# Hybrid attention block on one core: the near-distance bias moves from TensorE to VectorE's copy, and the inverse root to the split of y

## What is computed

```python
def block(args):
    i, qb = args
    dist = _block_dist(i, s)
    bias = rel_bias[_t5_bucket(jnp.maximum(dist, 0))]
    bias = jnp.moveaxis(bias, -1, 0).astype(jnp.float32)
    logits = jnp.einsum('bhqcd,bhkcd->bchqk', qb, k).astype(jnp.float32) * scale + bias
    logits = jnp.where(dist >= 0, logits, NEG)
    p = jax.nn.softmax(logits, axis=-1)
    a = p[:, 0] - lam * p[:, 1]
    return jnp.einsum('bhqk,bhkd->bhqd', a, v32)
...
o_a = _rmsnorm(o_a, diff_head_norm[l]) * (1.0 - lam_init)
...
y = y * jax.nn.silu(gate)
```

## Time and profile before

| | |
|---|---|
| median of 3 runs | 2624.19 us (2621.52 to 2629.36) |
| profiled execution | 2637.26 us, span of its instructions 2635.5 us |
| granted clock of PE, mean | 0.977 |
| PE, PEld busy | 2381.7 us (90%), 1629.8 us (62%) |
| DVE, ACT, POOL busy | 1725.6 us (65%), 1606.3 us (61%), 1335.5 us (51%) |
| diff stages (PE's scores of the kind diff) | 461 to 605, 985 to 1148, 1525 to 1680, 2065 to 2235 us |

### The profile page before, as it was taken

The page is one execution under the profiler, slowest core; times in us unless marked ns, Lnnn a source line. Parts: engine busy times, 40 slices in busy tenths (PEclk is TensorE's granted clock), DMA queues, the critical chain, the costliest instruction groups (busy, mean ns, idle before and its releaser), DMA issues. The chain is left out here.

```text
span 2635.5 us, 72425 instructions
## 1 busy us (share of the span) xinstructions
PE 2381.7 (90%) x27166; PEld 1629.8 (62%) x27166; DVE 1725.6 (65%) x4545; ACT 1606.3 (61%) x4373; POOL 1335.5 (51%) x2128
## 2 busy tenths in 40 slices
PE   5699999999999999979989999799899996799998
PEld 4576666666766666658666665586666654544443
DVE  7646689886556898866559988665588896311121
ACT  5456888566577886656678866566788665311221
POOL 6435555666575566666665666656756455100000
PEclk9799999999999999989999999899999998899999
DMA  6369998745699888356998983558998833764341
GB/s 195 95 119 154 158 160 151 143 87 104 136 181 169 156 143 163 69 107 135 172 171 155 142 167 74 93 123 164 178 158 145 154 69 57 192 167 104 89 112 48
DMA packets 987800, 353.05 MB, mean 134 GB/s; under 512 B 833956, under 2 KB 972204, under 8 KB 987436
## 3 DMA queue, kind: packets, MB, share of 16 engines
q1 hardware_dynamic: 980856, 330.58, 65.4%
q0 software_dynamic: 6592, 17.83, 2.5%
HBM read 72.38 MB, written 35.23 MB: 41 GB/s over the span
## 5 line engine op out<-in xcount | busy, mean ns | idle before, releaser
L1588 POOL TENSOR_TENSOR rows<-rows 128x512 f16<-128x512 f32 (+3 forms) x864 | 861.0, 1011 | 681.1 <-ACT rows L1514 674.9
L1345 PE MATMUL job<-wt,big 128*128 128x128 f16 x10752 | 682.8, 220 | 2.8 <-DVE planes L1603 1.9
L1345 PE MATMUL job<-big,wt 128*128 128x512 f16 x2688 | 665.8, 381 | 10.5 <-PEq L768 5.1
L1345 PEld LDWEIGHTS job<-wt,big 128*128 128x128 f16 x10752 | 628.9, 98 | 46.1 <-DVE planes L1603 3.0
L1514 ACT CAST rows<-rows 128x512 f16<-128x512 f32 (+3 forms) x864 | 458.2, 544 | 242.2 <-DMA rows<-rows 192.8
L1411 PE MATMUL mixed<-values,rows 128*128 128x64 f16 (+1 forms) x8544 | 428.9, 201 | 103.1 <-DMA rows<-rows 79.7
L1411 PEld LDWEIGHTS mixed<-values,rows 128*128 128x128 f16 x8544 | 378.0, 99 | 224.9 <-DMA rows<-rows 118.5
L1535 ACT ACTIVATE rows<-rows,neg_max 128x512 f32<-128x512 f32 (+3 forms) x704 | 445.6, 635 | 109.1 <-DVE neg_max L1649 108.9
L1393 PE MATMUL scores<-stack 128*128 128x512 f16 (+3 forms) x1600 | 435.2, 351 | 42.0 <-DVE rows L1641 31.9
L1641 DVE TENSOR_SCALAR_CACHE_REDUCE rows<-scores 128x512 f32<-128x512 f32 (+3 forms) x704 | 398.6, 590 | 89.4 <-POOL rows L1588 66.5
L1345 PEld LDWEIGHTS job<-big,wt 128*128 128x128 f16 x2688 | 246.6, 98 | 255.6 <-issue 13.5
(11 more groups left out here) (157 smaller groups left out, 2784.0 us busy)
## 6 DMA issues: line engine op xcount, KB each, us to landing
stack<-planes SPq DMA_DIRECT2D x160, 192.0 KB
ws<-w_in SPq DMA_DIRECT2D x56, 512.0 KB, 4.8
y_halves<-y_out_halves SPq DMA_DIRECT2D x64, 256.0 KB, 2.7
rows<-rows SPq DMA_TRANSPOSE x864, 3.3
rows<-x SPq DMA_DIRECT2D x16, 512.0 KB, 5.8
temps<-w_out POOLq DMA_DIRECT2D x64, 128.0 KB, 3.4
out_weight_halves<-temps POOLq DMA_DIRECT2D x64, 128.0 KB, 3.7
big<-out_weight_halves SPq DMA_DIRECT2D x16, 512.0 KB, 10.6
```

Of the source, the lines that this page charges most:

```text
L1345: last = nc.tensor.matmul(dst, lhs, rhs, start=(k0 == 0 and q == 0), stop=(k1 == KT and q == len(pairs) - 1))
L1588: nc.gpsimd.tensor_tensor(halves_of(tau, 1, w), scored(plan.chunk_at(g, m, k0), 0, w), halves_of(tau, 0, w), ALU.subtract).then_inc(low_po ...
```

## The change

The bias is added by DVE: a chunk is copied in up to two pieces, the far one by `tensor_scalar` as before and the near one by `tensor_tensor_reduce`, which adds the fp32 bias from `near_f` and takes the maximum. The three bias matmuls per near chunk, the buffer `near` and `split_near` go. `take` goes: `square` and `post` read the accumulator itself, and the next step's `mix` waits for `post`, as after the other kinds. `post` no longer multiplies by the root; `y_hi` and `y_low` do it as their scale, where the constant 0.5/64 was. The root, its variance, its sum of squares and its first guess get two places each, so `variance` and `inverse_root` wait for steps two back. Three one-element `scalar_tensor_tensor` of DVE (one in `combine`, two in `variance`) become `tensor_scalar`. The planner's numbers are all set anew (of `RANK` only PE's are shown).

```diff
--- before.py
+++ after.py
...
-    "pe": {"mix": 4.37083, "score": 4.93189, "gate": 5.45902, "project": 6.22450},
...
+    "pe": {"mix": 3.42686, "score": 5.99980, "gate": 6.18532, "project": 7.37012},
...
-                need = [("turn", tau)] + ([self.taken_by(g - 1)] if g and at == 0 else [])
+                need = [("turn", tau)] + ([("post", g - 1)] if g and at == 0 else [])
...
         def y_scale(g):
+            if KINDS[g] == "diff":
+                return root[:, DIFF_STEP[g] % 2:DIFF_STEP[g] % 2 + 1]
...
-                            sp.wait_ge(near_step, 5 * lane)
+                            sp.wait_ge(s_free, soft_count(plan.last_chunk[args[0] - len(KIND_ORDER)]))
...
-                        if kind == "diff" and i == 0:
-                            pe.wait_ge(near_step, 5 * (UNIT[t].lane + 1))
...
-                    if kind == "diff":
-                        first = max(c, (i - 1) * P)
-                        if first < c + w:
-                            at, width = first - c, c + w - first
-                            off = first - (i - 1) * P
-                            for a in range(3):
-                                parts.append((at, width, ident_b[:, :], near[:, a, off:off + width]))
...
-                        if KINDS[g - 1] == "diff":
-                            pe.wait_ge(o_copied, DIFF_STEP[g - 1] + 1)
-                        else:
-                            pe.wait_ge(posted, g)
+                        pe.wait_ge(posted, g)
...
-                    if op == "take":
-                        act.wait_ge(pv_done, mixed(g))
-                        if DIFF_STEP[g]:
-                            act.wait_ge(posted, g if KINDS[g - 1] == "diff" else LAST_DIFF[g] + 1)
-                        nc.scalar.copy(o_copy[:, :], o_bank[:, 0:P]).then_inc(o_copied, 1)
                     if op == "y_hi":
                         act.wait_ge(posted, g + 1)
+                        if KINDS[g] == "diff":
+                            act.wait_ge(root_step, (DIFF_STEP[g] + 1) * ROOT)
...
-                        act.wait_ge(o_copied, DIFF_STEP[g] + 1)
-                        nc.scalar.activation(junk[:, :], o_copy[:, :], ACT.Square, accum_out=sc[:, 6:7]) \
+                        d = DIFF_STEP[g]
+                        act.wait_ge(pv_done, mixed(g))
+                        if d >= 2:
+                            act.wait_ge(var_ready, (d - 1) * VAR)
+                        nc.scalar.activation(junk[:, :], o_bank[:, 0:P], ACT.Square, scale=P ** -0.5,
+                                             accum_out=sc[:, 10 + d % 2:11 + d % 2]) \
                             .then_inc(squared, 1)
...
-                    v, y, a, b = sc[:, 2:3], root[:, 0:1], root[:, 1:2], root[:, 2:3]
+                    v, y, a, b = sc[:, 8 + d % 2:9 + d % 2], root[:, d % 2:d % 2 + 1], root[:, 2:3], root[:, 3:4]
                     pool.wait_ge(var_ready, (d + 1) * VAR)
+                    if d >= 2:
+                        y_split(pool, DIFF_ROWS[d - 2])
...
+                def copies(g, c, w):
+
+                    first = (plan.steps[g][1] - 1) * P if KINDS[g] == "diff" else c + w
+                    cut = min(max(first - c, 0), w)
+                    return [(a, b) for a, b in ((0, cut), (cut, w)) if b > a], cut
+
                 def soft_chunk(g, n, m, c, w):
                     r = (2 * g + m) % ROWS
+                    t, i = plan.steps[g]
+                    at = sum(len(copies(g, c0, w0)[0]) for _, r0, c0, w0 in plan.chunks[g] if r0 == m and c0 < c)
                     dve.wait_ge(s_full, n + 1)
                     row_free(dve, n)
-                    nc.vector.tensor_scalar(scored(n, 0, w), s_bank[n % S_BANKS][:, 0:w], 1.0,
-                                            -3.0e38, ALU.mult, ALU.max,
-                                            accum_out=mx[:, r, c // BANK:c // BANK + 1]).then_inc(s_free, 1)
+                    cuts, cut = copies(g, c, w)
+                    if i == 0 and KINDS[g] == "diff":
+                        dve.wait_ge(near_landed, 16 * (UNIT[t].lane + 1))
+                    for q, (a, b) in enumerate(cuts):
+                        peak = mx[:, r, at + q:at + q + 1]
+                        if a < cut:
+                            last = nc.vector.tensor_scalar(scored(n, a, b), s_bank[n % S_BANKS][:, a:b], 1.0,
+                                                           -3.0e38, ALU.mult, ALU.max, accum_out=peak)
+                        else:
+                            off = c + a - (i - 1) * P
+                            last = nc.vector.tensor_tensor_reduce(scored(n, a, b), s_bank[n % S_BANKS][:, a:b],
+                                                                  near_f[:, ::-1][:, off:off + b - a], 1.0, -3.0e38,
+                                                                  ALU.add, ALU.max, peak)
+                    last.then_inc(s_free, 1)
...
-                        nc.vector.scalar_tensor_tensor(sc[:, 1:2], sc[:, 0:1], neg_lam[:, 0:1], z0, op0=ALU.mult,
-                                                       op1=ALU.mult).then_inc(coef_step, 1)
+                        nc.vector.tensor_scalar(sc[:, 1:2], sc[:, 0:1], neg_lam[:, 0:1], z0, ALU.mult, ALU.mult) \
+                            .then_inc(coef_step, 1)
...
-                    z0, v = z_sum[:, col(g, 0)], sc[:, 2:3]
-                    nc.vector.scalar_tensor_tensor(sc[:, 7:8], z0, EPS, z0, op0=ALU.mult, op1=ALU.mult) \
-                        .then_inc(var_ready, 1)
+                    d = DIFF_STEP[g]
+                    var = d * VAR
+                    z0, v, floor = z_sum[:, col(g, 0)], sc[:, 8 + d % 2:9 + d % 2], sc[:, 7:8]
+                    seed = root_i[:, d % 2:d % 2 + 1]
+                    if d >= 2:
+                        dve.wait_ge(root_step, (d - 1) * ROOT)
+                    nc.vector.tensor_scalar(floor, z0, z0, EPS, ALU.mult, ALU.mult).then_inc(var_ready, 1)
...
-                    nc.vector.scalar_tensor_tensor(v, sc[:, 6:7], 1.0 / P, sc[:, 7:8], op0=ALU.mult,
-                                                   op1=ALU.add).then_inc(var_ready, 1)
-
+                    dve.wait_ge(squared, d + 1)
+                    nc.vector.tensor_scalar(v, sc[:, 10 + d % 2:11 + d % 2], floor, None, ALU.add).then_inc(var_ready, 1)
...
-                    if kind == "diff":
-                        dve.wait_ge(o_copied, DIFF_STEP[g] + 1)
-                        dve.wait_ge(root_step, (DIFF_STEP[g] + 1) * ROOT)
-                        nc.vector.scalar_tensor_tensor(y, o_copy[:, :], root[:, 0:1], gate, op0=ALU.mult, op1=ALU.mult) \
-                            .then_inc(posted, 1)
-                        return
                     dve.wait_ge(pv_done, mixed(g))
-                    if kind == "stick":
-                        nc.vector.scalar_tensor_tensor(y, o_bank[:, 0:P], 0.5 / W_SCALE, gate, op0=ALU.mult,
-                                                       op1=ALU.mult).then_inc(posted, 1)
+                    if kind in ("stick", "diff"):
+                        if kind == "diff":
+                            dve.wait_ge(squared, DIFF_STEP[g] + 1)
+                        nc.vector.scalar_tensor_tensor(y, o_bank[:, 0:P], 0.5 / W_SCALE if kind == "stick" else 1.0, gate,
+                                                       op0=ALU.mult, op1=ALU.mult).then_inc(posted, 1)
...
-                def split_near(t):
-                    at = 5 * UNIT[t].lane
-                    dve.wait_ge(near_landed, 16 * (UNIT[t].lane + 1))
-                    if UNIT[t].lane:
-                        dve.wait_ge(s_full, plan.last_chunk[t - len(KIND_ORDER)])
-                    for a in range(3):
-                        nc.vector.tensor_copy(near[:, a, :], near_f[:, ::-1]).then_inc(near_step, 1)
-                        if a < 2:
-                            dve.wait_ge(near_step, at + 2 * a + 1)
-                            nc.vector.tensor_tensor(near_f[:, :], near_f[:, :], near[:, a, ::-1], ALU.subtract) \
-                                .then_inc(near_step, 1)
-                            dve.wait_ge(near_step, at + 2 * a + 2)
```

More of the change, by code:

```diff
@@ L58 @@
 RANK = {
[L59 to L70 removed]
+    "pe": {"mix": 3.42686, "score": 5.99980, "gate": 6.18532, "project": 7.37012},
+    "act": {"beta": -1.02044, "convert": 0.09860, "square": 1.56409, "y_hi": 1.90013, "stick": 4.11322,
+            "job": 4.42739, "hi": 4.85840, "exp": 6.05197},
+    "dve": {"lo_dve": 1.52081, "weigh": 1.69925, "ylo": 1.93750, "combine": 2.12124, "low": 2.34038,
+            "post": 3.72902, "scan": 4.02979, "norm": 6.33521, "widen": 6.61046, "copy": 7.20142},
+    "pool": {"lo": 0.09877, "wo": 2.26711, "ylo_pool": 2.95644, "root": 4.79189},
+    "sp": {"stacks": -0.49115, "store": 1.06927, "pairs": 1.90869, "sums": 2.46883, "turn": 2.93844,
+            "strip": 7.81310, "near_in": 13.10196},
+}
+AHEAD = {"mem": 1.00000, "stick": 0.75620, "diff": 0.14564, "forget": 0.68448}
+SLACK, LATE = 17.35582, 11.80560
 MARGIN = {
```

(20 more changed lines are left out.)

68 lines of the change are left out of this document (24 added, 44 removed).

## The result

The changed kernel took **2602.45 us** (median of 4 runs, 2597.89 to 2605.17) beside 2626.77 (2621.52 to 2629.36) of the kernel before on the same chip: ratio 0.9908, 95% interval 0.9885 to 0.9931. That is 24 us less; the forecast was 47 us less.

The account below looks back on a forecast made before the run. PE, busy 90% of the span, was taken as the bound. From the 2624.19 us median, -40.4 (bias matmuls) - 13 (VectorE's relief) + 6 (moved waits) = -47.4 gave 2577 us; range 2550 to 2612.

Parts of the forecast that it names:

- second case: Rival, 0.20: VectorE gives nothing back, as small tensor_scalars still wait for POOL or add-and-reduce is dear; 2590, up to 2610.
- The bias matmuls at 40.4 us: Diff stages on PE: removing 456 bias matmuls, 95,232 columns at 0.424 ns, saves 40.4 us; ends 20 and 66.2.
- No change: Rival, 0.06: the chain score, copy, exp, combine, transpose, mix sets each diff step, so freed time is waiting; about 2622.
- VectorE's relief at 13 us: Diff stages: 58 us less work on DVE shortens PE's 38.7 us of waits for copies by a third, 13 us.
- (b): DVE's chunk copies: chunks straddling the near tiles' border are cut in two, 88 more instructions, costing 8 us in all.
- (c): DVE's 152 near pieces: add-and-reduce taken to cost no more than the plain copy; other end 30 us.
- (d): DVE's three one-element operations per diff step, as tensor_scalar at 0.154 us: 79.4 us become 29.6, 49.8 us less.
- (e): DVE's y product, reading PSUM and no longer the root: 34.2 us become 18.0 at 0.281 us each, 16.2 us less.
- The waits that move: First mix matmul after a diff step now waits for square and product, not ACT's copy: adds 6 us; ends 0 and 32.
- The replanned order: Job parts newly placed around PE's 7.98 us bubble before the mem stage: taken as 0, with 15 us either way.
- Slower: Rival, 0.07: the next mix waits for the product queued behind exp and copy, 1.8 us later; 2629; decides from 0.83 us a step.
- The signs named in advance: PE busy some 40 us lower, DVE 58; variance operations 150 to 160 ns; PE's product wait under 10 us, copy waits about 26.

Follow-up runs that it names:

- run 1: Kernel before without its 456 bias matmuls, nothing else touched, so the near-distance bias is left out: 2611.75 us, ratio 0.9938.
- run 12: Kernel before with bias added by VectorE, small sums as tensor_scalar, root at y's split, take removed, 63 operations moved in the old order: 2822.74 us, 1.0743.
- run 3: Kernel before with only the three one-element operations per diff step turned into tensor_scalar: 2614.64 us, ratio 0.9941.
- run 5: Kernel before, in its old order, with bias added by VectorE and the three small sums as tensor_scalar, nothing else: 2591.95 us, ratio 0.9851.
- run 2: Kernel before, in its old order, with only the bias part changed (VectorE adds the bias as it copies, two bias buffers): 2609.36 us, ratio 0.9930.
- version 9: Kernel before with bias added by VectorE, small sums as tensor_scalar and root at y's split; take kept, old order: 2588.92 us, ratio 0.9843.

## Why the prediction was wrong

The sign, the range (2550 to 2612) and the band of the second case (2590 to 2610) held the time. That case held it by luck: of its mechanism, small sums that still wait for POOL or a dear add-and-reduce, nothing came. The forecast was 25 us too low; it promised 47 us and the change gave 24, and two terms carry that.

- **The bias matmuls at 40.4 us: the first step that failed.** As time they gave 16 us alone (run 1), below even the lower end of 20. As work the figure was high too: PE's busy time fell by 31.4 us in run 1 and by 26 to 40 in the other profiles without these matmuls, run 12 apart. Busy time of PE was read as path because PE was at 91%; as far as the waits show, in the diff stages the chain score, copy, exp, combine, mix sets the pace for part of the time: PE's waits for copies rose by 14 us (58.4 to 72.1). That was the rival given 0.06 ("No change"), half true.
- **VectorE's relief at 13 us** was about right: the small sums alone gave 15 (run 3), and 21 on top of the bias part (run 5 against run 2). Bias and relief together gave 39 to 41 (runs 5, 9), where the two terms said 53.4, so 12 to 14 us are missing, and they are the bias matmuls'. The reason given, that the stalls stand right ahead of copies, held: in run 3 PE's waits for copies fell by 15 us. The 38.7 us of such waits were counted to 2240 us in the last stage; to 2235, where the stage ends, they are 31.7, which changes nothing here.
- **(b) and (c)**: right. 418 and 285 ns are the copy's line, and run 2 equals run 1. **(d)**: the 154 ns was too low for sums that read a pointer (203, 214, 273 ns: 44 us, not 29.6), but the rival behind it didn't come. None of them was held up in 64 executions each (at most 274 ns, at L1674), though 44 (L1698), 44 (L1701) and 31 (L1674) of them began while a POOL operation ran; the old L1688 took up to 1153. The Trainium skill (VectorE: DVE Perf Modes, Mode 2×_2P; SBUF — State Buffer, Who interferes with whom), as the prediction read it, would let such a sum wait for GpSimd; in this trace no one-element `tensor_scalar` did. **(e)**: right, 282 ns.
- **"The waits that move" (6 us) and "The replanned order" (0)** were priced apart, and that is the second failed step. They are one trade. In the changed kernel the mix's wait for the product measured 1.3 us, less than forecast, because the order was built to avoid it; that order costs 23 us. With the 6 that the missing take gives back in it, the trade costs 17, 11 more than the two terms held together (6 + 0, with 15 either way for the order). The bound of the rival "Slower", 0.83 us a step, was the right one to compute: in the old order it is 3.6 us in 56 steps, and the kernel is slower by 195. It counted the wait alone, though; in run 12 the lower clock behind such waits added 57 us. And the rival put it down to an exp on ACT and one copy on DVE (1.8 us a step); what stood ahead of the product was DVE's whole queue of a step.
- The signs named in advance: PE's busy time in this profile, the near pieces and the product's wait came as said; DVE fell by 49 us and not 58. Neither sign of being wrong came, above 2612 us or 20 us more idle time of PE (253.8 before, 251.8 after). The variance's sums took 203 and 214 ns, above the 150 to 160, and PE's waits for copies, which were to fall, rose from 58.4 to 76.1 us over the whole kernel. That last one was the sign of the miss.

Not tried: a second accumulator bank in place of the take (the kernel holds 4 score, 3 job and 1 mix bank), the changed kernel's order with the root at `post`, and numbers searched for version 9, which at 0.9843 is 17 us faster than the change and keeps the take.

## What to carry to other kernels

Removing a copy that frees a buffer early doesn't only save the copy: it ties the next producer to the last reader, at that reader's place in its engine's queue. Price it by what stands ahead of the reader in the order (3.6 us a step here, for a 0.26 us copy on an engine with room), or by what the order loses when the reader is moved forward. Such a wait can cost more than its length: here PE was also busy 57 us longer for the same matmuls, at a lower granted clock. And when an engine at 90% loses work inside a chain, try the bare removal first: here it returned 16 us where the columns removed were priced at 40.

## What was not expected of the hardware

- A one-element tensor_scalar with pointers in SBUF took 196 to 274 ns in all of 192 executions, 119 of which began while a POOL operation ran; scalar_tensor_tensor in the same places took 147 to 1153, and the first of them, L1688, at most 155 where POOL was at rest. The change of form alone was worth 15 us.
- Add with a second operand, maximum and copy in one instruction ran at the plain copy's time: 418 ns against 420 at 128 x 256, with one operand in PSUM and one, reversed, in SBUF.
- ACT's copy with a scale from a pointer took 396 ns on average where the same copy with a constant scale took 308:

```profile
L1504 ACT ACTIVATE y_out_halves<-y_f 128x128 f16<-128x128 f32 x192 | 59.2, 308 | 18.9 <-DVE y_f L1738 12.9 <-DVE y_f L1731 5.4
...
L1504 ACT ACTIVATE y_out_halves<-y_f,root 128x128 f16<-128x128 f32 x64 | 25.3, 396 | 46.4 <-POOL root L1541 35.0 <-issue 10.8 <-DVE y_f L1731 0.4
```
